# A three-block sequence model in one kernel: where the sum of squares is finished, where its rows are issued, and where weight splits stand in VectorE's queue

## The reference

```python
for l in range(2):
    h = h + 0.5 * swiglu(rmsnorm(h))          # 1024 -> 2816 -> 1024
    h = h + hybrid_mixer(rmsnorm(h))          # mLSTM, retention, gated delta rule, then w_out
    h = h + 0.5 * swiglu(rmsnorm(h))
h = rmsnorm(h)
proj = rmsnorm(h) @ w_in                      # second block: gates, SSM and recurrent inputs
h = h + (sig(g0) * (ssm(proj) @ w1) + sig(g1) * (lru(proj) @ w2)) @ w_out
h = h + swiglu(rmsnorm(h))
return rmsnorm(h)
```

## Time and profile before

| | |
|---|---|
| median of 3 runs | 3385.09 us (3383.19 to 3385.43) |
| the profiled execution | 3385.09 us, its span 3383.3 us |
| mean granted clock of TensorE | 0.992 of full speed |
| TensorE busy | 97% of the span |
| VectorE, ScalarE busy | 51%, 38% |
| DMA, mean | 85 GB/s |

### The profile page before, as it was taken

One profiled execution on the slowest core, in us unless ns is written; L12 is line 12 of the kernel. 1 busy time (PEld: TensorE's weight loads), 2 busy tenths in 40 slices (PEclk: granted clock), 3 DMA queues, 4 the chain that ended last, 5 costly groups with the idle time before them and its releaser, 6 DMA issues.

```text
span 3383.3 us, 38790 instructions
## 1 busy us (share of the span) xinstructions
PE 3296.6 (97%) x15294; PEld 2691.3 (80%) x15294; DVE 1726.6 (51%) x2424; ACT 1271.0 (38%) x1870; POOL 30.5 (1%) x62
## 2 busy tenths in 40 slices
PE   8999999899999999999999999999999999999998
PEld 6888776688888888877668888877888877888887
DVE  4443455765443444344675544455555577454433
ACT  3222334443222322233444322345455466332221
POOL 0000000000000000000000000000000000000000
PEclk9999999999999999999999999999999999999999
DMA  4233321113233233332211323321211222332331
GB/s 145 97 97 92 102 75 59 38 50 107 96 96 95 96 99 95 96 96 73 66 44 36 113 99 96 93 86 57 69 63 62 78 90 89 107 100 94 100 92 64
DMA packets 107397, 288.05 MB, mean 85 GB/s; under 512 B 22913, under 2 KB 34177, under 8 KB 107217
## 3 DMA queue, kind: packets, MB, share of 16 engines
q1 hardware_dynamic: 91696, 278.70, 25.6%
q10 hardware_dynamic: 14208, 2.63, 0.4%
q0 software_dynamic: 1312, 4.25, 0.4%
HBM read 282.64 MB, written 2.88 MB: 84 GB/s over the span
## 4 chain that ended last, share of the span: by engine, by line
PE 85%; DVE 8%; ACT 4%; issue 2%; ACTq 1%; DMA 1%; DVEq 0%; SPq 0%
PE ps L759 26%; PE ps L761 25%; PE ps L760 25%; PE ps L768 2%; DVE wl L1932 1%; DVE mf L2118 1%; ACT wh L1338 1%; PE ps L1069 1%; PE ps L1225 1%; PE ps L1064 1%; ACT L1329 1%; PE ps L1207 1%; PE ps L1221 0%; ACTq L1630 0%; PE ps L773 0%
## 5 line engine op out<-in xcount | busy, mean ns | idle before, releaser
L1338 ACT ACTIVATE wh<-raw 128x1024 fp32r<-128x1024 f32 (+3 forms) x581 | 567.6, 977 | 1692.1 <-PE ps L761 1658.7
L759 PE MATMUL ps<-hnh,wh 128*128 128x512 f32 x2712 | 1082.2, 399 | 16.1 <-DVE mf L2095 7.1
L761 PE MATMUL ps<-hnh,wl 128*128 128x512 f32 x2712 | 1062.0, 392 | 0.0
L760 PE MATMUL ps<-hnl,wh 128*128 128x512 f32 x2712 | 1061.4, 391 | 0.0
L1932 DVE TENSOR_TENSOR wl<-raw,wh 128x1024 fp32r<-128x1024 f32 (+3 forms) x581 | 651.9, 1122 | 603.9 <-ACT wh L1338 600.9
L759 PEld LDWEIGHTS ps<-hnh,wh 128*128 128x128 f32 x2712 | 512.3, 189 | 140.6 <-issue 22.8
L761 PEld LDWEIGHTS ps<-hnh,wl 128*128 128x128 f32 x2712 | 512.2, 189 | 108.5
L760 PEld LDWEIGHTS ps<-hnl,wh 128*128 128x128 f32 x2712 | 512.8, 189 | 105.8 <-issue 3.1
L759 PE MATMUL ps<-mr,wh 128*128 128x512 f32 x1300 | 511.2, 393 | 5.9 <-DVE mf L2480 4.3
L761 PE MATMUL ps<-mr,wl 128*128 128x512 f32 x1300 | 507.4, 390 | 0.0
L760 PE MATMUL ps<-mr,wh 128*128 128x512 f32 x1300 | 507.4, 390 | 0.0
(11 more groups left out here) (293 smaller groups left out, 2407.2 us busy)
## 6 DMA issues: line engine op xcount, KB each, us to landing
raw<-in_w_in SPq DMA_DIRECT2D x140, 512.0 KB, 3.5
raw<-in_ffn_w_gate SPq DMA_DIRECT2D x88, 512.0 KB, 3.5
raw<-in_ffn_w_up SPq DMA_DIRECT2D x88, 512.0 KB, 3.5
raw<-in_ffn_w_down SPq DMA_DIRECT2D x64, 512.0 KB, 3.5
raw<-in_w_ffn_in SPq DMA_DIRECT2D x44, 512.0 KB, 3.5
raw<-in_ffn_w_down SPq DMA_DIRECT2D x32, 384.0 KB, 3.1
raw<-in_w_out SPq DMA_DIRECT2D x32, 256.0 KB, 2.6
raw<-in_w_out_ssm SPq DMA_DIRECT2D x32, 256.0 KB, 2.5
```

The source lines that it names most:

```text
L759: self.e.matmul(out, ah, bh, start=start, stop=False, skip_group_check=shared)
L760: self.e.matmul(out, ah, bl, start=False, stop=False, skip_group_check=shared)
L761: m = self.e.matmul(out, al, bh, start=False, stop=stop, skip_group_check=shared)
L1338: self.e.activation(k.spl[u % NSPL][0][:, 0:n], k.raw[u % NRAW][:, 0:n], ACT.Copy).then_inc(k.w_hi, 1)
```

## The change

1. The sum of squares is closed by TensorE. VectorE no longer adds the square of tile 7. `sums(0)` sums what VectorE has accumulated of tiles 0 to 6; it is issued when tile 6's late work is due, or with `sums(1)` in a short round. `sums(1)` adds the sums of tile 7's square straight from ScalarE's buffer into the same PSUM columns.
2. `root_rows` is issued two slices into the second product and not four.
3. `end_taps` doesn't flush before it issues the remaining taps.
4. The flush behind `take_yl` and those behind `take_branch` go.
5. `gate_acc` of the previous gate stands ahead of `take_branch` of this one, in `branch_acc` and in the last loop.

```diff
@@ -330,7 +330,6 @@
 
     def end_taps(self):
         if self.taps:
-            self.flush()
             for _ in self.taps:
                 pass
         self.taps = None
@@ -385,7 +384,7 @@
         b = B_PROJ[self.q % 2] if bank is None else bank
         for n, _ in enumerate(self.pieces(xs, ready, bank)):
             self.beside()
-            if n == 2:
+            if n == 1:
                 self.root_rows()
         return b
 
@@ -403,7 +402,7 @@
         return self.r if self.r < LAST else self.r - 1
 
     def sq_n(self, i):
-        return 8 * (self.r - 1) + i, 7 * (self.r - 1) + i - 1
+        return 8 * (self.r - 1) + i, 6 * (self.r - 1) + i - 1
 
     def h_new(self, i, gain):
         if self.r == LAST:
@@ -420,8 +419,12 @@
     def run_late(self):
         if self.late is not None:
             i, self.late = self.late, None
+            if i == 6 and not self.short:
+                self.sums(0)
             if i == 7:
-                self.sums()
+                if self.short:
+                    self.sums(0)
+                self.sums(1)
                 if self.r == LAST:
                     self.two_roots()
                 else:
@@ -722,10 +724,9 @@
         parts = [k.pair(L_HI[i], L_LO[i]) for i in range(8)]
         for i in range(8):
             self.product_h()
-            self.take_branch(8 + i, gate[i % 2], 8 + i)
-            self.flush()
             if i == 0:
                 self.gate_acc(7)
+            self.take_branch(8 + i, gate[i % 2], 8 + i)
             self.finish()
             self.product(y, lambda j: (k.scan_a.at(j // 2, f"hi{j % 2}"), k.scan_v.at(j // 2, f"lo{j % 2}")))
             self.take_mix(i, gate[i % 2], parts[i])
@@ -734,10 +735,9 @@
     def branch_acc(self, i):
 
         self.product_h()
-        self.take_branch(i, self.k.gate_of(i), i)
-        self.flush()
         if i > 4:
             self.gate_acc(i - 1)
+        self.take_branch(i, self.k.gate_of(i), i)
 
     def build(self):
         self.start()
@@ -880,16 +880,22 @@
                               start=start and j == 0, stop=stop, skip_group_check=True)
         return m
 
-    def sums(self):
-
-        k = self.k
-        _, v = self.sq_n(7)
-        self.wait_ge(*k.sq_v.at(v, "acc"))
-        m = self.sum_of(0, k.tmp(2), True, True)
+    def sums(self, last):
+
+        k = self.k
+        a, v = self.sq_n(7 if last else 6)
+        if last:
+            self.wait_ge(*k.sq_a.at(a, "sq"))
+        else:
+            self.wait_ge(*k.sq_v.at(v, "acc"))
+        m = self.sum_of(0, k.tmp(3 if last else 2), not last, last == 1)
         if self.r == LAST:
-            self.wait_ge(*k.two_s.at(6, "acc"))
-            m = self.sum_of(4, k.tmp(1), False, True)
-        m.then_inc(*k.hn_p.up(self.r - 1, "sum"))
+            if last:
+                self.wait_ge(*k.two_a.at(7, "sq"))
+            else:
+                self.wait_ge(*k.two_s.at(5, "acc"))
+            m = self.sum_of(4, k.slot(S_SQ) if last else k.tmp(1), False, last == 1)
+        m.then_inc(*k.hn_p.up(2 * (self.r - 1) + last, "sum"))
 
     def rstd(self):
         k = self.k
@@ -1412,7 +1418,7 @@
         k, e = self.k, self.e
         A, V = k.tr_a, k.tr_v
         self.load(ACT.Sqrt)
-        self.wait_ge(*k.hn_p.at(self.r - 1, "sum"))
+        self.wait_ge(*k.hn_p.at(2 * (self.r - 1) + 1, "sum"))
         e.activation(k.rc2[0], k.ps[B_SUM][:, 0:4], ACT.Sqrt, bias=k.cl("eps"), scale=1.0 / D).then_inc(*A.up(0, "first"))
         self.wait_ge(*V.at(0, "whole"))
         e.activation(k.rc2[1], k.rc2[1], ACT.Sqrt, bias=k.cl("eps"), scale=1.0 / D).then_inc(*A.up(0, "second"))
@@ -1969,7 +1975,7 @@
 
     def add_square(self, i):
         k = self.k
-        if i:
+        if 1 <= i <= 6:
             n, v = self.sq_n(i)
             acc = k.tmp(2)
             self.wait_ge(*k.sq_a.at(n, "sq"))
```

## The result

The changed kernel takes 3408.4 us (median of 4, 3402.84 to 3410.76) against 3385.26 us (3383.19 to 3386.12): ratio 1.0064, 95% interval 1.0052 to 1.0077, so +18 to +26 us. The forecast was 3395.8 us in a range from 3389 to 3402. The direction was right and the size was not.

A forecast was written before the change was run, and what follows sets the result against it. TensorE, busy 97% of the span, was taken to bound the kernel. 6.4 + 1.8 - 1.0 + 2.2 + 0.9 + 0.8 - 0.4 = +10.7 us on 3385.1 gave 3395.8 us, range 3389 to 3402.

The forecast's parts named there:

- Part 1: Normalisation rounds 1 to 7: eight added `sum_of` calls cost TensorE 0.80 us each, +6.4 us; the saved addition gains nothing there.
- Part 2: Earlier row matmuls wait for the square root's chain: +1.8 us in rounds 3 and 7, -1.0 us in 1 and 4.
- Part 3: Taps ahead of the weight split: VectorE's next work later at convolution groups' ends, less a state-space entry gain; +2.2 us.
- -0.5 us for the one entry: Entry to the state-space block: h's scalings cover the tap, so taps end 0.5 us sooner ahead of a wait.
- part 3's other term: Convolution groups' ends: VectorE idles longer for ScalarE's tap, 0.54 us at about five places, 2.7 us.
- Parts 4 and 5: Recurrent stage: split delays `take_yl(1)`, +0.9 us; branch 7: eviction behind a multiplication, +0.8 us after less low-clock time.
- the 1.6 us booked: Branch 7's eviction: later by 0.6 us here, 0.6 us from branch 5's swap and 0.4 us from the recurrent stage.
- Part 6: Tail, round 8: last sums wait for ScalarE's square instead of VectorE's eighth addition and start earlier, -0.4 us.

The follow-up runs named there:

- changed, without part 3: Changed kernel with the flush put back ahead of the remaining taps in `end_taps`; 3390.19 us, ratio 1.0015 to the kernel before.
- changed, flush in `finish`: Changed kernel with one flush written ahead of the taps in `finish()` alone; 3394.91 us, ratio 1.0032 to the kernel before.
- part 3 alone: Kernel before with only the flush ahead of the remaining taps removed from `end_taps`; 3402.22 us, ratio 1.0045.
- part 1 alone: Kernel before with only the second group of sums and no VectorE addition for tile 7; 3389.65 us, ratio 1.0013.
- part 2 alone: Kernel before with only `root_rows` issued two slices into the second product; 3387.88 us, ratio 1.0007.
- parts 4 and 5 alone: Kernel before with only the flushes behind `take_yl` and `take_branch` removed and `gate_acc` ahead of `take_branch`; 3386.24 us, ratio 1.0005.
- before, no flush in `finish`: Kernel before without the flush ahead of the taps in `finish()` alone, the mixers' groups keeping theirs; 3394.99 us, ratio 1.0027.

## Why the prediction was wrong, by its own steps

**Part 1** was right in mechanism and size. A call costs 0.8 to 0.95 us, no wait of TensorE's in the full rounds went with VectorE's addition, and the part alone measured +4.4 us (1.4 to 7.4), against 6.4 - 0.4 = 6.0.

**Part 2** was right in mechanism; its size (+0.9 us forecast) is below what the runs can tell. Timeline of round 1 in the changed kernel, for the earlier trace rows:

```profile
389.26 0.95 PE L879 MATMUL ps<-cst,mf 128*128 128x1 f32 x8
...
390.59 1.28 ACT L1335 ACT_TABLE_LOAD   x1
391.89 0.27 ACT L1444 ACTIVATE small<-ps,col 128x4 f32<-128x4 f32 x1
...
392.19 0.18 DVE L2049 RECIPROCAL small<-small 128x4 f32<-128x4 f32 x1 [6.01 <-ACT small L1444]
...
392.42 1.16 PE L778 MATMUL ps<-cst,small 128*128 128x128 f32 x8 [0.70 <-DVE small L2049]
...
393.61 0.69 DVE L2053 COPY mf<-ps 128x512 f32<-128x512 f32 x1 [1.25 <-PE ps L778]
```

From the sums to the copy it is 4.35 us where it was 4.76, and the row matmuls wait 0.70 us behind the table load. Rounds 3, 4 and 7 repeat the 0.70; rounds 2 and 5 have no wait.

**Part 3 failed, and in one step**: "the split, which the next product flushes at once, still stands ahead of the next work. What is queued behind it is ...". I asked who waits for VectorE's next work and not who waits for the flushed low half itself. Behind the mixers' groups nobody does for three products. At the entry of the state-space groups TensorE does, within the first product. There I booked -0.5 us for the one entry with a wait in the trace before (for ScalarE's copy, 1.47 us; it did vanish) and did not count the other three, where nothing waited. What the runs put in the place of this -0.5 us is +9.1 us (6.1 to 12.2) with the flush gone there alone, and 10.8 us (3408.4 against 3394.9, by the ratios 0.0032 of 3385) with it put back in the changed kernel. The waits of part 3's other term, the mixers' groups, were as forecast. The changed kernel's timeline for the earlier trace rows:

```profile
510.57 2.32 DVE L2124 SCALAR_TENSOR_TENSOR mf<-mf,col,mf 128x511 f32<-128x511 f32 x3 [1.07 <-ACT mf L1483]
512.81 1.22 DVE L1938 TENSOR_TENSOR wl<-raw,wh 128x1024 fp32r<-128x1024 f32 x1
...
513.94 0.68 DVE L2403 TENSOR_TENSOR mf<-mf,ps 128x512 f32<-128x512 f32 x1
...
515.86 1.12 PE L1117 MATMUL ps<-mf,cst 128*128 128x512 f32 x2 [2.62 <-ACT mf L1676]
```

The 1.07 us of VectorE and the 0.54 us on TensorE's wait (2.62 in place of 2.08) are the forecast numbers. Between the traces of the changed kernel without part 3 and with the flush in `finish`, which differ in these groups, TensorE's waits grow by 2.4 us (4.2 to 5.2, 4.7 to 5.2 and 1.3 to 2.2). The times differ by more: 5.7 us there, and 6.1 us between part 3 alone and its share in `finish` (0.0045 less 0.0027). With intervals of some 0.001 on each ratio this is not told apart from the 2.7 us booked, and it is not shown to be right either.

**Parts 4 and 5**: 1.7 us forecast and measured, with an interval from -1.4 to +4.7 us, so the agreement to the tenth is luck. The mechanism was right. At branch 7, for the earlier trace rows:

```profile
2879.03 0.67 DVE L2478 TENSOR_TENSOR mf<-mf,mf 128x512 f32<-128x512 f32 x1
2879.61 0.69 DVE L2486 TENSOR_TENSOR mf<-ps,mf 128x512 f32<-128x512 f32 x1
...
2880.36 0.79 PE L759 MATMUL ps<-mr,wh 128*128 128x512 f32 x1 [5.20 <-DVE mf L2486]
```

and the window around it:

```profile
2879.50:2884.00 4.50, 3.65 (x9) 2.87 (x10) 4.33 (x7) 2.65 (x4) 0.00 (x0) 0.50 0.27 82
```

The multiplication stands ahead of the eviction. The wait grew by 0.9 us, less than the 1.6 us booked, as TensorE itself came to the place later: the product before now waits 0.40 us for branch 6's eviction, where the trace before has no such wait. The clock is low behind it, as it was.

**Part 6** was right in sign and small in size:

```profile
3384.51 0.94 PE L879 MATMUL ps<-cst,mf 128*128 128x1 f32 x8
...
3387.38 0.63 ACT L1402 ACTIVATE mf<-h 128x512 f32<-128x512 f32 x1 [14.34 <-DVE h L2064]
...
3388.06 1.05 PE L879 MATMUL ps<-cst,mf 128*128 128x1 f32 x8 [2.10 <-ACT mf L1402]
```

The last product's last matmul starts at 3384.28 and the span ends 14.2 us later, 15.1 us before: -0.9 us for -0.4. The sums start 0.34 us earlier against the last product (3.78 us behind it and not 4.12), as forecast. They also ran in 1.05 us and not in 1.42, by where the clock fell, within them before (granted clock 0.70) and behind them here (1.00), which was not forecast.

**Beyond the waits**: the profiled execution is +15.2 us, the median +23.1 us (+21.7 us by the ratio). The difference is the clock of the one profiled execution, by the estimate above: it lost some 7 us less to the low level than the kernel before did in its own, and 15.2 + 7 makes 22 us. Over all their executions the two kernels lose about the same, 28 and 27 us. So the changed kernel is slower by its waits and its added matmuls, some 21 us of them, and not by more falls than the kernel before. The same split for the parts (us; a mean clock is listed to 0.001 for each execution, so take these to a few us, and the rows of five executions as the roughest):

| | executions | measured | of it low clock | the rest |
|---|---|---|---|---|
| part 1 alone | 11 | +4.4 | -1.8 | +6.2 |
| part 2 alone | 11 | +2.4 | +3.1 | -0.7 |
| part 3 alone | 5 | +15.2 | +6.9 | +8.4 |
| parts 4 and 5 alone | 11 | +1.7 | 0.0 | +1.7 |
| changed, without part 3 | 11 | +5.1 | -5.6 | +10.7 |
| changed, flush in `finish` | 5 | +10.8 | -3.7 | +14.5 |
| before, no flush in `finish` | 11 | +9.1 | -0.6 | +9.7 |
| changed | 19 | +21.7 | +1.2 | +20.5 |

The changed kernel without part 3 had fewer falls than the kernel before, and part 3 brings them back. Of the three traces with its four waits, two show a fall at two of them; why the other parts have fewer is open, and only one execution of each kernel has a trace.

## What to carry to other kernels

When an instruction is moved back in an engine's queue, ask two questions, who waits for what stands behind it and who waits for the thing itself, and ask the second at every place where the helper runs, not only where the trace before shows a wait. A place without a wait may be one that is met with 0.15 us to spare, as here; look for consumers that use several buffers at once, since they use up the slack of all. And before two traces are compared, compare their clocks: here one profiled execution had some 7 us less of the low level than the other, half as much as their spans differ by (15.2 us).

## What the runs showed of the hardware

Behind the same wait of 2.14 us at the same place, TensorE's granted clock fell to its lower level in two traces (part 3 alone; the kernel before without the flush in `finish`) and stayed up in a third (the changed kernel). Behind the wait of 2.78 us at the place before it was the same. The clock also fell with TensorE never idle, behind 2.73 us of 24 matmuls of one column, at one of the two short rounds that had them. The Trainium skill (TensorE: Matmul & The Clock Gate, "HAM oscillation — how this bites in real kernels") tells of a loop in which the clock falls at every one of its waits for a DMA, which are of 3 to 5 us. Here shorter waits were enough, in some executions, and one fall had no wait ahead of it.
